# Placing rotations, a key projection, index heads and stick logits inside weight tiles of the second block's mixers

## The chip, the cores and the metric

The kernel is one program on one core of a Trainium2 chip. The metric is the device time of one execution in microseconds, the median of the runs. Everything is float32; the large products are made of float32r parts (a weight split in a high and a low part, an activation split likewise, three products summed).

## The reference, cut to what matters

Two transformer blocks of depth 2 run one after the other on 256 tokens of width 1024. The change touches the mixer of the second block (`hybrid_mixer`), which runs once for each of its two layers, between two feed-forward parts:

```python
(q_a, k_a, v_a, f_a, q_b, k_b, v_b, q_c, c_kv, q_i, k_i, w_i, gates) = split(h @ w_in)
y_a = forgetting_attention(q_a, k_a, v_a, f_a + b_forget)     # 6 heads; cumsum of log_sigmoid(f)
y_b = stick_breaking_attention(q_b, k_b, v_b)                 # 5 heads; logits z = q k^T
k_c, v_c = split(rmsnorm(c_kv, g_kv) @ w_kv_up)               # the key's up-projection
q_c, k_c = partial_rope(q_c), partial_rope(k_c)               # rotations
q_i = partial_rope(q_i)                                       # 4 index heads
k_i = partial_rope(rmsnorm(k_i, g_idx_k))                     # one index key
score = sum_h w_i[h] * relu(q_i[h] @ k_i^T)                   # index heads
y_c = attention over the top 64 keys of score (8 at a time in 8 rounds)
merged = sigmoid(gates) * (y @ w_up) ; return merged @ w_out
```

## The kernel before, in words

Features stand on the 128 partitions and tokens along the free axis. A weight piece (128 x 2048, 1 MB, or smaller) comes by DMA into one of four ring slots. ScalarE copies it in two halves to `w_hi` (float32r, two buffers; L1664), VectorE subtracts in two halves to get `ring_lo` (L2161). Both do this for the next piece when they handle the first tile of the current one (`ahead`, called at the head of `act_feat` and `dve_feat`). ScalarE may overwrite a `w_hi` buffer once TensorE has begun the piece that follows its old content.

A tile is one output chunk of 128 features by 256 tokens: 24 matmuls of 256 columns, issued by `product` (L1195) in the order 8 pairs of (high weight x high activation, high weight x low activation), then 8 of low weight x high activation. Most pieces hold two tiles. TensorE waits for `w_hi` before the first and for `ring_lo` before the 17th matmul of a tile. Tiles go to PSUM banks 0 to 2 in turn.

An ordered list of items (`add(kind, ...)`) is written out by hand. Each engine walks this one list from top to bottom and does its own part of each item: TensorE, ScalarE, VectorE and GpSimd are each strictly in that order. `fill(bank)` reserves the next use of a PSUM bank: TensorE waits in `room(f)` until the bank's former user is taken out, the engine that reads it waits in `full(f)` and counts `psum_taken` when done. Rotations, the key's up-projection (`kvup`), index heads and the head norm's sums and spread share T_BANKS (5 and 6), stick logits share S_BANKS (3 and 4).

An item with `inside=True` is left out of TensorE's walk alone; TensorE issues it instead within a tile, ahead of the matmul whose number stands in that tile's `mids`. The other engines still do it at its place in the list.

The parts of the mixer's list that matter (a chunk is a tile, `chunks(i)` a piece of two tiles):

- `chunks(0)`, `chunks(1)`: the latent, the index key, the index queries. `tok vb`: values. Then `head_squares`.
- `chunks(2)` (features 12, 13 of `q_c`), with `head_sums` between its tiles (TensorE L1442, ScalarE's root, VectorE's reciprocal L2505).
- `fox_ls`: the forget gate's log-sigmoid. VectorE adds the bias (L2640), ScalarE does Abs, Exp, Ln (L1975 to L1977), and VectorE waits for that at L2643.
- `chunks(3)`, with `head_spread` between its tiles (TensorE L1460, into both T banks; VectorE L2515).
- `chunks(4)` (QX, 9); between its tiles `kvup` (L1570, L1573), the rotations of the index key and of both index query chunks (L1470; VectorE L2526, L2527, L2529), and `key_twice` (a ScalarE copy, L1981, after the key's rotation). After its second tile four more rotations.
- the single tile of chunk 10, `index(0)`: four index heads against 128 keys (TensorE L1593, ScalarE relu L1989, VectorE L2670 and L2672).
- `chunks(5)` with `index(1)` (256 keys), the caps and stick logits 0 and 1 (`stick_z`: L1602, L1603; VectorE L2699; ScalarE Abs and Exp) between its tiles; stick logits 2 and 3 behind it; `chunks(6)` with stick logit 4 between its tiles; `chunks(7)`; `tok va` (L1426).

Of the kernel before, what the change touches and what calls it, by code (L numbers as in the profile page):

```python
# [148 lines left out]
class Plan:  # L149
# [15 lines left out]
    def linear(self):  # L165
        self.lin += 1
        if (self.lin - 1) % LIN == self.held:
            self.lin += 1
        return self.fill((self.lin - 1) % LIN)
# [10 lines left out]
    def count(self, name, n=1):  # L180
        self.counts[name] = self.counts.get(name, 0) + n
        return self.counts[name]
# [13 lines left out]
def hybrid_kernel(nc, xt, vec_d, con_d, tables_d, rpb, w, out):  # L196

    with ExitStack() as ctx:
# [399 lines left out]
                if i < len(steps) + 3:  # L598
                    g["last"] = add("att", steps=steps, i=i, inside=inside)

        def rope(chunks, block, need=(), inside=False):
            return add("rope", block=block, need=need, tb=turned_by if block == 1 else turned_by2, inside=inside,
                       chunks=[(b, a, low, linear() if inside else fill(T_BANKS[i % 2]), count("rope")) for i, (b, a, low) in enumerate(chunks)])

        def head_norm(chunks, root, kv=False, low=(0,) * 5):

# [337 lines left out]
        def second_block(l):  # L944
# [15 lines left out]
            def fc(c):  # L960
                return feats[f"2f{l}", c]

            def index(t):
                add("index", t=t, after=plan.counts["rope"], twice=plan.counts["key_twice"], fs=[fill(T_BANKS[h % 2]) for h in range(4)],
                    n=[count("relu") for _ in range(4)])

            foxes = []

# [5 lines left out]
            zs = []  # L974

            def stick_z(*hs):
                for h in hs:
                    zs.append(fill(S_BANKS[h % 2]))
                    add("stick_z", h=h, f=zs[-1], n=5 * l + h, after=fc(10))

            accs = []

# [9 lines left out]
            hn = head_norm([(feat2, CKV * S, S, v("g_kv", l), fc(CKV)), (feat2, KX * S, S, v("g_idx", l), fc(KX))], hroot2, True, (0, DH))  # L992
            head_squares(hn, 0, 1)
            t = chunks(2)
            next(t)
            head_sums(hn)
            run_all(t)
            add("fox_ls", l=l, after=feats[f"vb{l}", 0], n=count("fox_ls"))
            t = chunks(3)
            next(t)  # L1000
            head_spread(hn, 0, 1)
            run_all(t)
            t = chunks(4)
            next(t)
            kv = [fill(b) for b in (T_BANKS[0], T_BANKS[1], V_BANK)]
            add("kvup", l=l, fs=kv, need=hn["spread"][1])
            kv_last[0] = kv[-1]
            rope([(feat2, KX * S, DH), (feat2, QI * S, 0), (feat2, (QI + 1) * S, 0)], 2, need=(hn["spread"][1],))
            add("key_twice", n=plan.counts["rope"] - 2, k=count("key_twice"))
            run_all(t)  # L1010
            rope([(feat2, 12 * S, 0), (feat2, 13 * S, 0), (feat2, QX * S, DH), (kc2, 0, 0)], 2, need=(fc(QX), kv[0]))
            run_all(feat(f"2f{l}", [(0, P, cols(5, 0, P))], [10], S, length=KC * P))
            index(0)
            t = chunks(5)
            next(t)
            index(1)
            add("index_caps")
            stick_z(0, 1)
            run_all(t)
            add("index_round")  # L1020
            stick_z(2, 3)
            t = chunks(6)
            next(t)
            add("index_round")
            stick_z(4)
            run_all(t)
            add("index_round")
            t = chunks(7)
            next(t)
            add("stick_ln", n=5 * l, zs=zs)  # L1030
# [112 lines left out]
        def _(pe):  # L1143
# [21 lines left out]
            def product(fs, n, groups, fresh=None, need=None, at_col=0, mids={}, more=False, hold=False, odd=None):  # L1165

                for f in fs:
                    room(f)  # L1170
                left = [3 * sum(len(terms) for _, terms in groups)] * len(fs)
                first, at_mm = left[0], 0
                for p, terms in groups:
                    hi_w, lo_w = w_hi[p.s % 2], ring_lo[p.slot]
                    by_chunk = fresh is not None or need
                    if by_chunk:
                        order = [(*parts, t, k) for t in terms for parts in (("hi", "hi"), ("lo", "hi"), ("hi", "lo")) for k in range(len(fs))]
                    else:
                        order = [("hi", part, t, 0) for t in terms for part in ("hi", "lo")] + [("lo", "hi", t, 0) for t in terms]
                    for wpart, part, (at, hi, lo, rows, c), k in order:  # L1180
                        h = 1 if not by_chunk or at[k] + P > p.length // 2 else 0
                        for part_of, seen, ready in (("hi", hi_seen, w_hi_ready), ("lo", lo_seen, w_lo_ready)):
                            if wpart == part_of and seen.get(p.n, -1) < h:
                                seen[p.n] = h
                                pe.wait_ge(ready, 2 * p.s + h + 1)
                        if fresh is not None and wpart == "hi" and k == 0:
                            pe.wait_ge(h_hi_ready if part == "hi" else h_lo_ready, fresh - KC + c + 1)
                            if part == "lo" and c % 2 and odd is not None:
                                pe.wait_ge(odd_lo_ready, odd + c // 2 + 1)
                        if need and part == "hi" and wpart == "hi" and k == 0:  # L1190
                            pe.wait_ge(need[0], need[1] + c + 1)
                        if at_mm in mids:
                            dict(sums=pe_sums, spread=pe_spread, att=pe_att)[mids[at_mm][0]](mids[at_mm][1])
                        at_mm += 1
                        mm = pe.matmul(ps[fs[k].bank][:, at_col:at_col + n], (hi_w if wpart == "hi" else lo_w)[0:rows, at[k]:at[k] + P],  # L1195
                                       hi if part == "hi" else lo, start=left[k] == first, stop=left[k] == 1)
                        left[k] -= 1
                        if left[k] or more:
                            if not hold:
                                run(p, mm)  # L1200
                        else:
                            mm.then_inc(psum_full[fs[k].bank], 1)
# [381 lines left out]
            def pe_index(st):  # L1584
                t = st["t"]
                pe.wait_ge(rope_ready, st["after"])
                pe.wait_ge(key_twice, st["twice"])
                nk = (t + 1) * P
                for h, f in enumerate(st["fs"]):
                    room(f)  # L1590
                    a = slice(DH * (h % 2), DH * (h % 2) + DH)
                    o = (QI + h // 2) * S + t * P
                    pe.matmul(ps[f.bank][:, 0:nk], feat2[a, o:o + P], feat2[a, (KX if h % 2 else KI) * S:][:, 0:nk], start=True, stop=True)\  # L1593
                        .then_inc(psum_full[f.bank], 1)
# [544 lines left out]
        def _(dve):  # L2139
# [520 lines left out]
            def dve_index(st):  # L2660
                t = st["t"]
                nk = (t + 1) * P
                sc = score[:, t * S:t * S + nk]
                for h, (f, n) in enumerate(zip(st["fs"], st["n"])):
                    taken(f)
                    iw = vb2[:, t * 384 + 326 + h:t * 384 + 327 + h]
                    rl = relu_t[:, n % 2 * S:n % 2 * S + nk]
# [3 lines left out]
                    else:  # L2671
                        ins = dve.tensor_scalar(sc, rl, iw, None, ALU.mult)  # L2672
                    ins.then_inc(relu_used, 1)
                dve.wait_ge(relu_used, st["n"][-1])

            def by_t(do_t):
                for t in range(2):
# [173 lines left out]
```

## Time and profile before

| | us |
|---|---|
| median of 3 runs (2461.84 to 2463.28) | 2462.05 |
| the profiled execution, its own time | 2463.62 |
| its span, first to last instruction | 2461.8 |
| TensorE (PE) busy | 2410.3, 98% |
| VectorE (DVE) busy | 1557.8, 63% |
| ScalarE (ACT) busy | 1221.9, 50% |
| GpSimd (POOL) busy | 363.2, 15% |
| mean granted TensorE clock | 0.993 |

The span and the busy times are those of one profiled execution; 1.8 us of its time lie outside the span. A busy time is the union of an engine's instructions. Matmuls overlap in the records: in a stream of tiles one starts each 0.12 us and its record is 0.28 us long, so lengths of stretches are best read from starts.

### The profile page before, as it was taken

What the parts mean: (1) busy time and instruction counts of PE and PEld (TensorE: products, weight loads), DVE (VectorE), ACT (ScalarE), POOL (GpSimd) and SP (SyncE); (2) the same over time, 40 slices, a digit from 0 to 9 for tenths busy, and PEclk for the clock granted to TensorE, in tenths of its full rate; (3) what the DMA queues carried; (4) which work ended last, traced back from release to release, by engine and by line L of the source; (5) the groups of instructions that cost most, each with busy time, mean ns of one, the idle gap of its engine ahead of it and who ended that gap; (6) DMA issues with size and microseconds to landing.
All of it is one profiled execution on the core that took longest, in us unless ns stands there. A gap on an engine that the chain in (4) does not pass through costs nothing.

```text
span 2461.8 us, 36798 instructions
## 1 busy us (share of the span) xinstructions
PE 2410.3 (98%) x14494; PEld 2062.9 (84%) x14494; DVE 1557.8 (63%) x2659; ACT 1221.9 (50%) x2224; POOL 363.2 (15%) x340
## 2 busy tenths in 40 slices
PE   8999999999999999999999999999999999999998
PEld 6865678878888777888888889998888888999887
DVE  5234455663455445677678667677767767757875
ACT  4344453322223445566556545566656654547653
POOL 0333422000001325100100000240010010024000
PEclk9999999999999999999999999999999999999999
DMA  6334423444444422455555553355565564435554
GB/s 274 130 112 155 154 86 120 154 162 137 154 167 142 146 93 96 137 171 178 192 200 183 176 173 129 123 179 188 172 203 187 175 192 147 136 114 201 188 173 135
DMA packets 88603, 389.95 MB, mean 158 GB/s; under 512 B 15024, under 2 KB 27600, under 8 KB 58352
## 3 DMA queue, kind: packets, MB, share of 16 engines
q1 hardware_dynamic: 81232, 356.07, 42.5%
q0 software_dynamic: 7200, 31.52, 3.7%
q8 instruction: 116, 1.90, 0.3%
q14 instruction: 55, 0.45, 0.1%
HBM read 386.52 MB, written 1.05 MB: 157 GB/s over the span
## 4 chain that ended last, share of the span: by engine, by line
PE 90%; DVE 4%; ACT 3%; DMA 1%; issue 1%; SPq 0%; POOL 0%; DVEq 0%; POOLq 0%; ACTq 0%
PE ps L1195 40%; PE ps L1235 37%; PE ps L1426 3%; PE ps L1489 2%; PE ps L1500 2%; PE ps L1515 2%; DVE ring_lo L2161 2%; DMA prob_t<-w_mod 1%; ACT w_hi L1664 1%; PE ps L1326 1%; PE ps L1341 0%; ACT logits L1897 0%; PE ps L1470 0%; DMA ring<-w_w_in 0%; PE ps L1360 0%
## 5 line engine op out<-in xcount | busy, mean ns | idle before, releaser
L2161 DVE TENSOR_TENSOR ring_lo<-ring,w_hi 128x1024 fp32r<-128x1024 f32 (+4 forms) x708 | 774.1, 1122 | 218.7 <-ACT w_hi L1664 216.4
L1664 ACT ACTIVATE w_hi<-ring 128x1024 fp32r<-128x1024 f32 (+4 forms) x708 | 634.2, 944 | 267.9 <-PE ps L1195 175.1
L1195 PE MATMUL ps<-h_hi,w_hi 128*128 128x256 f32 (+1 forms) x1632 | 502.4, 334 | 2.4 <-issue 1.6
L1195 PE MATMUL ps<-h_lo,w_hi 128*128 128x256 f32 (+1 forms) x1632 | 489.5, 326 | 1.5 <-DVE h_lo L2334 1.5
L1235 PE MATMUL ps<-h_hi,w_hi 128*128 128x512 f32 x1760 | 449.0, 395 | 2.2 <-DVE h_hi L2334 1.8
L1235 PEld LDWEIGHTS ps<-h_hi,w_hi 128*128 128x128 f32 x1760 | 318.3, 190 | 58.6 <-issue 2.8
L1195 PEld LDWEIGHTS ps<-h_hi,w_hi 128*128 128x128 f32 x1632 | 309.0, 191 | 39.0 <-issue 12.6
L1195 PEld LDWEIGHTS ps<-h_lo,w_hi 128*128 128x128 f32 x1632 | 309.5, 191 | 25.9 <-DVE h_lo L2334 1.7
L1195 PE MATMUL ps<-h_hi,ring_lo 128*128 128x256 f32 (+1 forms) x1632 | 305.1, 325 | 2.5 <-DVE ring_lo L2161 2.5
L1195 PEld LDWEIGHTS ps<-h_hi,ring_lo 128*128 128x128 f32 x1632 | 250.5, 191 | 27.7 <-DVE ring_lo L2161 3.0
L1235 PEld LDWEIGHTS ps<-h_hi,ring_lo 128*128 128x128 f32 x1760 | 244.6, 192 | 21.7 <-DVE ring_lo L2161 3.6
L1235 PE MATMUL ps<-h_hi,ring_lo 128*128 128x256 f32 x1760 | 252.4, 284 | 2.7 <-DVE ring_lo L2161 2.7
L2088 POOL TENSOR_SCALAR logits<-logits,stat 128x512 f32<-128x512 f32 (+2 forms) x140 | 161.4, 1166 | 562.6 <-DVE stat L2571 562.6
L1235 PE MATMUL ps<-hid_both,w_hi 128*128 128x512 f32 x880 | 226.2, 393 | 0.0
L2400 DVE TENSOR_TENSOR prob_t<-ps,prob_t 128x256 f32<-128x256 f32 x260 | 110.4, 424 | 174.9 <-ACT prob_t L1810 174.6
L2044 POOL TENSOR_TENSOR logits<-logits 128x256 f32<-128x256 f32 (+1 forms) x65 | 67.7, 1041 | 1000.5 <-ACT logits L1685 781.3
L1810 ACT ACTIVATE prob_t<-ps 128x256 f32<-128x256 f32 x260 | 99.5, 383 | 213.1 <-PE ps L1235 213.1
L1235 PEld LDWEIGHTS ps<-hid_both,w_hi 128*128 128x128 f32 x880 | 161.0, 189 | 30.6
L1897 ACT ACTIVATE logits<-logits,stat 128x512 f32<-128x512 f32 (+2 forms) x140 | 81.6, 584 | 188.0 <-DVE logits L2559 93.2
L1235 PE MATMUL ps<-hid_both,ring_lo 128*128 128x256 f32 x880 | 133.4, 283 | 0.0
L1235 PEld LDWEIGHTS ps<-hid_both,ring_lo 128*128 128x128 f32 x880 | 122.5, 191 | 5.7
L1836 ACT ACTIVATE prob_t<-prob_t 128x256 f32<-128x256 f32 x110 | 46.0, 418 | 109.0 <-DVE prob_t L2424 97.2
(298 smaller groups left out, 2905.3 us busy)
## 6 DMA issues: line engine op xcount, KB each, us to landing
ring<-w_ffn_in SPq DMA_DIRECT2D x132, 1024.0 KB, 4.8
ring<-w_ffn_out SPq DMA_DIRECT2D x96, 704.0 KB, 4.1
ring<-w_in SPq DMA_DIRECT2D x36, 1024.0 KB, 4.9
ring<-w_w_in SPq DMA_DIRECT2D x26, 1024.0 KB, 4.9
bias_t<-w_mod POOLq DMA_DIRECT2D x24, 1024.0 KB, 5.4
ring<-w_mod SPq DMA_DIRECT2D x16, 1024.0 KB, 6.2
ring<-w_up SPq DMA_DIRECT2D x16, 576.0 KB, 3.8
ring<-w_pab SPq DMA_DIRECT2D x8, 1024.0 KB, 4.9
```

Of the source, the lines that this page charges most:

```text
L1195: mm = pe.matmul(ps[fs[k].bank][:, at_col:at_col + n], (hi_w if wpart == "hi" else lo_w)[0:rows, at[k]:at[k] + P], hi if part == "hi" else ...
L1235: mm = pe.matmul(ps[f.bank][:, 0:cols], wt[:, at + q * P:at + q * P + P], both[:, 0:cols], start=left[q] == n, stop=left[q] == 1, skip_gro ...
L1426: mm = pe.matmul(ps[f.bank][:, 0:st["n"]], at_T(part, c, T, t * P, P), wt[:, at:at + st["n"]], start=c == 0 and part is h_hi and not low, ...
L1489: pe.matmul(ps[f.bank][:, 0:sp_["nk"]], p["q"][a, t * P:(t + 1) * P], p["k"][a, k0:k0 + sp_["nk"]], start=True, stop=True).then_inc(psum_f ...
L1500: mm = pe.transpose(ps[f.bank][:, c * P:(c + 1) * P], logits[:, o:o + P], ident)
L1664: act.activation(w_hi[q.s % 2][:, h * n:(h + 1) * n], ring[q.slot][:, h * n:(h + 1) * n], ACT.Copy)\
L1810: act.activation(tmp[i][:, S:SQ], ps[f.bank][:, S:SQ], ACT.Copy).then_inc(half_out, 1)
L1897: act.activation(lg, lg, ACT.Exp, scale=-1.0, bias=stat[:, o:o + 1], accum_out=stat[:, 4 + o:5 + o])\
L2044: pool.tensor_tensor(sq_sum[:, o:n], sq_sum[:, o:n], sq[j % 2][:, o:n], ALU.add).then_inc(sq_added, 1)
L2088: pool.tensor_scalar(lg, lg, stat[:, 8 + (a % 2) * 2 + h:9 + (a % 2) * 2 + h], None, ALU.mult)\
L2161: dve.tensor_tensor(ring_lo[q.slot][:, c], ring[q.slot][:, c], plain(w_hi[q.s % 2][:, c]), ALU.subtract)\
L2400: dve.tensor_tensor(tmp[i][:, to:to + S], ps[f.bank][:, 0:S], tmp[i][:, S:SQ], ALU.add).then_inc(psum_taken[f.bank], 1)
```

## The change

It moves TensorE's part of these items into tiles, one or two at a stop, and with them the items' places in the list, which all engines follow:

- The rotations of the index queries go into the first tile of `chunks(2)` (ahead of matmuls 8 and 16), those of features 12 and 13 into the first tile of `chunks(3)`, `kvup` and the index key's rotation into the first tile of `chunks(4)`, those of the attention key and QX into its second tile.
- `index` now takes a list of heads: heads 0, 1 ahead of matmul 6 and heads 2, 3 ahead of matmul 16, in chunk 10's tile for the first 128 queries and in the first tile of `chunks(5)` for the others. It waits for the rotations up to the index key's alone.
- Stick logits 0, 1 go into the second tile of `chunks(5)`, 2, 3 into the first of `chunks(6)`, 4 into its second, each ahead of matmul 12.
- In the list each moved item stands ahead of its host tile's `feat` item, since it is added before `next(tile)`.
- `rope` takes the PSUM bank to use. The instructions themselves stay the same in number and shape.

```diff
-        def rope(chunks, block, need=(), inside=False):
+        def rope(chunks, block, need=(), inside=False, bank=None):
...
-            def index(t):
-                add("index", t=t, after=plan.counts["rope"], twice=plan.counts["key_twice"], fs=[fill(T_BANKS[h % 2]) for h in range(4)],
-                    n=[count("relu") for _ in range(4)])
+            def index(t, *hs):
+                return add("index", t=t, hs=hs, after=key_turned, twice=plan.counts["key_twice"], fs=[fill(T_BANKS[h % 2]) for h in hs],
+                           n=[count("relu") for _ in hs], inside=True)
+
+            def turned(chunk, bank, *need):
+                return rope([chunk], 2, need=need, inside=True, bank=T_BANKS[bank])
+
+            def among(tile, groups):
+
+                next(tile)
+                plan.items[-1]["mids"] = {at: [(it["kind"], it) for it in its] for at, its in groups.items()}
...
             t = chunks(2)
-            next(t)
+            among(t, {8: [turned((feat2, QI * S, 0), 0, fc(QI))], 16: [turned((feat2, (QI + 1) * S, 0), 1, fc(QI + 1))]})
             head_sums(hn)
             run_all(t)
             add("fox_ls", l=l, after=feats[f"vb{l}", 0], n=count("fox_ls"))
             t = chunks(3)
-            next(t)
+            among(t, {8: [turned((feat2, 12 * S, 0), 1, fc(12))], 16: [turned((feat2, 13 * S, 0), 0, fc(13))]})
             head_spread(hn, 0, 1)
             run_all(t)
             t = chunks(4)
-            next(t)
             kv = [fill(b) for b in (T_BANKS[0], T_BANKS[1], V_BANK)]
-            add("kvup", l=l, fs=kv, need=hn["spread"][1])
+            up = add("kvup", l=l, fs=kv, need=hn["spread"][1], inside=True)
             kv_last[0] = kv[-1]
-            rope([(feat2, KX * S, DH), (feat2, QI * S, 0), (feat2, (QI + 1) * S, 0)], 2, need=(hn["spread"][1],))
-            add("key_twice", n=plan.counts["rope"] - 2, k=count("key_twice"))
+            key = turned((feat2, KX * S, DH), 0, hn["spread"][1])
+            key_turned = plan.counts["rope"]
+            add("key_twice", n=key_turned, k=count("key_twice"))
+            among(t, {8: [up], 16: [key]})
+            among(t, {8: [turned((kc2, 0, 0), 1, kv[0])], 16: [turned((feat2, QX * S, DH), 0, fc(QX))]})
             run_all(t)
-            rope([(feat2, 12 * S, 0), (feat2, 13 * S, 0), (feat2, QX * S, DH), (kc2, 0, 0)], 2, need=(fc(QX), kv[0]))
-            run_all(feat(f"2f{l}", [(0, P, cols(5, 0, P))], [10], S, length=KC * P))
-            index(0)
+            among(feat(f"2f{l}", [(0, P, cols(5, 0, P))], [10], S, length=KC * P), {6: [index(0, 0, 1)], 16: [index(0, 2, 3)]})
             t = chunks(5)
-            next(t)
-            index(1)
+            among(t, {6: [index(1, 0, 1)], 16: [index(1, 2, 3)]})
             add("index_caps")
-            stick_z(0, 1)
+            among(t, {12: stick_z(0, 1)})
+            add("index_round")
+            t = chunks(6)
+            among(t, {12: stick_z(2, 3)})
+            add("index_round")
+            among(t, {12: stick_z(4)})
+            add("index_round")
             run_all(t)
-            add("index_round")
-            stick_z(2, 3)
-            t = chunks(6)
-            next(t)
-            add("index_round")
-            stick_z(4)
-            run_all(t)
-            add("index_round")
```

## Rows read from the trace of the kernel before

**Rows 1.** The page: busy time of each engine; the final chain's shares by line.
```profile
PE 2410.3 (98%) x14494; PEld 2062.9 (84%) x14494; DVE 1557.8 (63%) x2659; ACT 1221.9 (50%) x2224; POOL 363.2 (15%) x340
...
PE ps L1195 40%; PE ps L1235 37%; PE ps L1426 3%; PE ps L1489 2%; PE ps L1500 2%; PE ps L1515 2%; DVE ring_lo L2161 2%; DMA prob_t<-w_mod 1%; ACT w_hi L1664 1%; PE ps L1326 1%; PE ps L1341 0%; ACT logits L1897 0%; PE ps L1470 0%; DMA ring<-w_w_in 0%; PE ps L1360 0%
```

**Rows 2.** TensorE's waits, 1463 to 1492 us: line, releaser: us, times, longest.
```profile
PE ps L1593 <- ACT arena L1989: 0.8, 2, 0.5
PE ps L1470 <- DVE arena L2526: 0.7, 2, 0.5
```

**Rows 3.** Timeline, TensorE, layer 0's mixer: start, length, line, operands, count.
```profile
1447.86 0.28 PE L1195 MATMUL ps<-h_hi,w_hi 128*128 128x256 f32 x1
...
1457.34 0.70 PE L1460 MATMUL ps<-arena,con 32*128 32x256 f32 x4
...
1458.19 0.28 PE L1195 MATMUL ps<-h_lo,w_hi 128*128 128x256 f32 x1
...
1460.95 0.28 PE L1195 MATMUL ps<-h_hi,w_hi 128*128 128x256 f32 x1
...
1463.83 0.59 PE L1570 MATMUL ps<-arena,kvup 128*128 128x256 f32 x2
...
1499.93 0.34 PE L1426 MATMUL ps<-w_hi,h_hi 128*128 128x384 f32 x1
```

**Rows 4.** Timeline, TensorE, a rotation inside a values tile.
```profile
870.17 0.40 PE L1426 MATMUL ps<-w_hi,h_lo 128*128 128x512 f32 x1
870.41 0.59 PE L1470 MATMUL ps<-arena,tables 128*128 128x256 f32 x2
...
871.07 0.40 PE L1426 MATMUL ps<-w_hi,h_lo 128*128 128x512 f32 x1
```

**Rows 5.** Timeline, TensorE, stick logit 4 between tiles.
```profile
1489.30 1.12 PE L1195 MATMUL ps<-h_hi,ring_lo 128*128 128x256 f32 x8
1490.35 0.70 PE L1602 MATMUL ps<-arena 64*128 64x256 f32 x2
...
1491.42 0.28 PE L1195 MATMUL ps<-h_lo,w_hi 128*128 128x256 f32 x1
```

**Rows 6.** Timeline, TensorE, two heads' scores of the same shape as an index pair.
```profile
1546.00 0.70 PE L1489 MATMUL ps<-arena 64*128 64x256 f32 x4
...
1546.86 0.28 PE L1195 MATMUL ps<-h_lo,w_hi 128*128 128x256 f32 x1
```

**Rows 7.** Timeline, VectorE, layer 0's mixer (in brackets: idle before, releaser).
```profile
1450.19 2.36 DVE L2161 TENSOR_TENSOR ring_lo<-ring,w_hi 128x1024 fp32r<-128x1024 f32 x2 [2.14 <-ACT w_hi L1664]
...
1452.80 1.74 DVE L2505 RECIPROCAL arena<-arena 64x256 f32<-64x256 f32 x1
...
1454.91 0.16 DVE L2640 TENSOR_TENSOR small<-arena,vec 128x12 f32<-128x12 f32 x1
1458.50 0.17 DVE L2643 SCALAR_TENSOR_TENSOR arena<-small 128x12 f32<-128x12 f32 x1 [3.42 <-ACT small L1977]
...
1465.74 0.43 DVE L2526 TENSOR_TENSOR arena<-ps,tables 64x256 f32<-64x256 f32 x1 [0.70 <-PE ps L1470]
...
1466.99 0.42 DVE L2526 TENSOR_TENSOR arena<-ps,tables 128x256 f32<-128x256 f32 x1
```

**Rows 8.** Timeline, ScalarE, the same mixer.
```profile
1466.99 0.42 ACT L1981 ACTIVATE arena<-arena 64x256 f32<-64x256 f32 x1 [1.91 <-DVE arena L2529]
...
1478.74 2.00 ACT L1664 ACTIVATE w_hi<-ring 128x1024 fp32r<-128x1024 f32 x2
```

**Rows 9.** Stretches: from:to, us, PE busy (count), granted clock, DMA share, GB/s.
```profile
199.80:202.10 2.30, 0.07 (x3) 1.00 0.85 280
...
203.70:207.10 3.40, 3.40 (x10) 0.50 1.09 404
...
1253.20:1255.80 2.60, 0.11 (x2) 1.00 0.83 340
1255.80:1259.20 3.40, 3.40 (x21) 1.00 0.03 12
```

More of the change, by code:

```diff
@@ L599, in att @@
                     g["last"] = add("att", steps=steps, i=i, inside=inside)
-        def rope(chunks, block, need=(), inside=False):
+        def rope(chunks, block, need=(), inside=False, bank=None):
             return add("rope", block=block, need=need, tb=turned_by if block == 1 else turned_by2, inside=inside,
-                       chunks=[(b, a, low, linear() if inside else fill(T_BANKS[i % 2]), count("rope")) for i, (b, a, low) in enumerate(chunks)])
+                       chunks=[(b, a, low, fill(T_BANKS[i % 2] if bank is None else bank) if bank or not inside else linear(), count("rope")) for i, (b, a, low) in enumerate(chunks)])
         def head_norm(chunks, root, kv=False, low=(0,) * 5):
@@ L976, in stick_z @@
             def stick_z(*hs):
+                items = []
                 for h in hs:
                     zs.append(fill(S_BANKS[h % 2]))
-                    add("stick_z", h=h, f=zs[-1], n=5 * l + h, after=fc(10))
+                    items.append(add("stick_z", h=h, f=zs[-1], n=5 * l + h, after=fc(10), inside=True))
+                return items
             accs = []
@@ L1192, in product @@
                         if at_mm in mids:
-                            dict(sums=pe_sums, spread=pe_spread, att=pe_att)[mids[at_mm][0]](mids[at_mm][1])
+                            for what, it in mids[at_mm] if isinstance(mids[at_mm], list) else [mids[at_mm]]:
+                                dict(sums=pe_sums, spread=pe_spread, att=pe_att, rope=pe_rope, kvup=pe_kvup, index=pe_index,
+                                     stick_z=pe_stick_z)[what](it)
                         at_mm += 1
@@ L1588, in pe_index @@
                 nk = (t + 1) * P
-                for h, f in enumerate(st["fs"]):
+                for h, f in zip(st["hs"], st["fs"]):
                     room(f)
@@ L2663, in dve_index @@
                 sc = score[:, t * S:t * S + nk]
-                for h, (f, n) in enumerate(zip(st["fs"], st["n"])):
+                for h, f, n in zip(st["hs"], st["fs"], st["n"]):
                     taken(f)
@@ L2673, in dve_index @@
                     ins.then_inc(relu_used, 1)
-                dve.wait_ge(relu_used, st["n"][-1])
+                if st["hs"][-1] == 3:
+                    dve.wait_ge(relu_used, st["n"][-1])
             def by_t(do_t):
```

## The prediction, before the changed kernel ran

> **What bounds the kernel now.** I read the page's busy times first: TensorE works 98% of the span, and the final chain runs 77% of its time through the two tile lines [rows 1]. So time is won only where TensorE idles or loses columns, and lost as soon as it is made to wait. The second view is TensorE's waits over the stretch that the change touches: it idles 1.9 us there in each mixer, mostly for a T bank to be emptied by the rotation before or by a relu (the two rows shown make 1.5, two more 0.2 each) [rows 2]. The third is the timeline. A mixer's piece from `chunks(2)` to `tok va` lasts 1499.93 - 1447.86 = 52.07 us; a tile is 1463.83 - 1460.95 = 2.88, or 0.120 a matmul; 13 tiles make 37.44 and leave 14.63 for everything between them [rows 3]. Of that, `head_spread` costs 0.82 (its last slot before at 1457.13, second tile matmul after at 1458.19, less two ordinary slots of 0.12) [rows 3]; I estimate `head_sums`, as many instructions, at 0.75. Both stay. The six stops that the change dissolves cost 14.63 - 1.57 = 13.06. Layer 1's mixer is the same list, so all is counted twice.
>
> **What the moved matmuls cost inside tiles.** None is removed. A 128-row rotation inside a tile takes 871.07 - 870.17 = 0.90, less two slots of 0.23 there, 0.44 [rows 4]; I use 0.43, its columns alone. Five of them: 2.15. `kvup` I keep at 0.82. Stick logit 4 alone costs 1491.42 - 1490.14 (the start of the eighth `ring_lo` matmul) - 0.24 = 1.04, for 0.64 of columns (384, four passes at 2.4 GHz): a spell of 64-row operands in the stream costs 0.40 extra [rows 5]. No row shows a 64x64 rotation alone: from 0.54 (its pitch in a row of rotations) to 0.43 + 0.40 = 0.83; I take 0.83, nearest to how it will stand, for two 1.66. An index pair of 256 keys costs 0.83 by the score pair of the same shape, of 128 keys 0.21 less [rows 6]: four make 2.9. Stick logits 1.5, 1.5 and 1.04: 4.0. Sum 11.5. Bounds: 11.2 with the cheap rotation, and 12.4 from the other side (13.06 less the 1.9 of waits, plus three more 64-row spells at 0.40, six before and nine after). Taken: **-1.6 us a mixer** (-0.7 to -1.9).
>
> One rule speaks against the change. The Trainium skill, TensorEngine Tiling (Array Packing), Key Properties, says that a change of tiling mode drains TensorE. The 0.40 in rows 5 against nothing extra in rows 4 agrees with it. With switches free inside tiles, a mixer would be 3.6 cheaper still, and the result about 7 us lower.
>
> **What the new order makes late.** The moved items stand ahead of their host's `feat` item, so on VectorE and ScalarE they come before the next piece's split.
>
> (1) *`head_spread` waits for both T banks, and these now hold the rotations of features 12 and 13.* VectorE does these behind `fox_ls`, where it already sits idle 3.42 us for ScalarE's chain [rows 7]. That chain now starts later: the two index rotations in `chunks(2)` come first on VectorE. The second is issued at 1447.86 + 16 slots + 0.43 = 1450.21, done on TensorE about 0.6 later, and VectorE needs 1.2 for a rotation (1465.74 to 1466.99) [rows 7], so it is free at 1452.1 for the `ring_lo` that began at 1450.19. Everything behind it (two evictions, the 1.74 reciprocal, the bias add at 1454.91, the return at 1458.50) moves by 1.9: VectorE comes back at 1460.4, does rotation 12 from 1460.6 and the first operation of 13 from 1461.8, and bank 5 is free at 1462.25. TensorE reaches `head_spread` at 1457.34 + 4 x 0.43 = 1459.06. It waits **3.2 us**. Before, nothing on TensorE waited for `fox_ls`. Bounds 2.9 and 3.5 (rotations of 1.1 or 1.25 us).
>
> (2) *QX.* From the slot k of the key's rotation: TensorE done at k+0.74; VectorE from +0.87 to +2.1; then `key_twice`, which followed at once before (0.42) [rows 8], and only then ScalarE's split of chunk 10 (two halves of 0.6), to k+3.6; VectorE's second half, then QX's eviction, out at k+4.7. TensorE wants QX at k + 0.83 + 8 slots + 16 slots + 0.43 = k+4.1. Wait **0.7** (0.4 to 1.0).
>
> (3) *`w_hi` of `chunks(5)`.* ScalarE did this split (2.00 us [rows 8]) as chunk 10's tile began; now four relus come first. From the slot s of heads 2, 3: TensorE done at s+0.57, two relus to s+1.0, both halves at s+3.0. TensorE wants them at s + 0.61 + 8 slots = s+1.57. Wait **1.5** (1.3 to 1.7). The same order in the first tile of `chunks(5)` costs nothing, since the second tile's 2.88 + 1.5 hide it. `chunks(7)`'s split, behind stick logits 2 and 3 on ScalarE, has about 1 us in hand, and `tok va`'s about 0.4; for its second piece, where TensorE idles 0.55 already, I add **0.2**.
>
> Sum: -1.6 + 3.2 + 0.7 + 1.5 + 0.2 = **+4.0 a mixer, +8.0**. DMAs, SP and GpSimd: no transfer is moved; the ring's only get more time, and GpSimd has no part in the moved items.
>
> (4) *The clock.* After TensorE stood almost idle for 2.3 us at 199.8, the granted clock was 0.50 from 203.7 to 207.1; after a pause as long at 1253.2 it stayed 1.00 [rows 9]. Of the five pauses or clusters with over 2 us idle in this trace four were followed by such a spell. Pauses of 1 to 1.6 us mostly were not. A 3.2 us wait is longer than any single one so far, so I count a spell in each mixer. 3.4 us at 1.2 GHz hold 16 tile matmuls (256 columns: 0.213) where 28 would fit at 0.120: 1.5 us lost, **+3.0** for two. Bounds: none (0) and two a mixer (+6).
>
> Total 8.0 + 3.0 = 11 us. Against the profiled execution: 2463.62 + 11 = 2474.6. The median of the runs shown is 1.6 lower, so **2473.0**.
>
> **Rivals.**
> - *The waits, but no low clock* (or one spell in all): 2470 to 2471.5. For it: the pause at 1253. Against: the other four.
> - *More is late*: a second spell after the 1.5 us wait, or `chunks(7)`'s split misses its 1 us: 2475 to 2478. For it: one pause of only 1.04 us near 1238 preceded a spell. Against: six of 1.1 to 1.6 didn't.
> - *Other side: VectorE gets to rotations 12 and 13 in time.* One mechanism: the T banks are empty when TensorE reaches `head_spread` at 1459.06. It needs `fox_ls` to return before 1457.2 instead of 1460.4, by having its chain overlap. Then the 3.2 and the clock spells fall away, and if the relus also run ahead so that (3) hides, only -1.6 + 0.7 a mixer is left: 2460; with all waits gone, 2459. For it: the 1.9 us of waits before really go [rows 2]. Against: VectorE's idle 3.42 stands in the list between the two [rows 7], and the point is missed by 3 us.
> - *The waits are half of what I count* (say (1) at 1.5 with no spell, (3) at 1): about 2462 to 2465, near no change. For it: my sums chain many steps. Against: each is in-order work with durations from rows.
>
> **How the numbers follow.** The forecast (three waits, a spell in each mixer) 0.45; no or one spell 0.24; more late 0.09; near no change 0.12; the other side 0.10. About 0.2% (4.9 us) is what a measurement of this kernel tells from none: 2457.1 to 2467.0. Slower: 0.45 + 0.24 + 0.09 = 0.78; same: 0.12 and half of the other side, whose 2459 to 2460 lies within, 0.17; faster, where more waits go than I see, 0.05. The range runs from 2466, under the no-spell case with the waits at their low bounds, to 2477, the forecast with one more spell or the high bounds; it leaves out about 2 in 10.
>
> **What would show it.** In the changed kernel's timeline: TensorE idle about 3 us ahead of `head_spread`, released by VectorE's rotation (L2526's successor); 0.7 ahead of QX's rotation, released by its eviction; 1.5 ahead of the first tile of `chunks(5)`, released by ScalarE's `w_hi`. The mixer's stretch goes from 52.1 to some 56, or 57.6 with a spell; the mean granted clock falls by two spells in 2462 us, about 0.001. The old waits at the rotations, relus and stick logits are gone. If `head_spread` starts without a wait, the main step is wrong; if TensorE waits there but the clock stays 1.00, only (4) is.

## The result, and the profile after

| | before | after |
|---|---|---|
| median of 5 runs each, us | 2463.28 (2461.84 to 2463.81) | 2471.3 (2469.98 to 2474.19) |
| ratio, with its 95% interval | | 1.0038 [1.0027, 1.0049] |
| the profiled execution, its own time, us | 2463.62 | 2471.3 |
| span, us | 2461.8 | 2469.5 |
| mean granted TensorE clock | 0.993 | 0.992 |

The changed kernel is slower by 8.0 us by the medians (6.7 to 12.1 by the interval of the ratio) where 11 were forecast. Its median lies 1.7 us under the predicted 2473.0 and inside the range.

On the page TensorE's busy time barely moves (2410.3 before, 2411.9 here), so the page alone does not show what the change did [rows 1]:

```profile
PE 2411.9 (98%) x14494; PEld 2062.4 (84%) x14494; DVE 1555.3 (63%) x2659; ACT 1221.2 (49%) x2224; POOL 363.6 (15%) x340
```

The length to compare is a mixer's stretch: the time from its first matmul of `tok vb` to its first of `tok va`, in layer 0 and in layer 1. First the kernel before, then the changed one (us; busy PE, PEld, DVE, ACT, POOL; granted clock, DMA share, GB/s):

```profile
1440.50:1499.93 59.43, 57.56 (x426) 52.78 (x425) 44.14 (x91) 31.46 (x52) 0.00 (x0) 1.00 0.44 142
```

```profile
1437.68:1502.05 64.37, 59.02 (x426) 53.73 (x425) 43.65 (x90) 30.70 (x52) 0.00 (x0) 0.97 0.41 131
2047.47:2111.83 64.36, 59.01 (x426) 53.72 (x425) 43.64 (x90) 30.71 (x52) 0.00 (x0) 0.97 0.41 131
```

The stretch grew by 4.94 us. TensorE is idle for 5.35 us of it (64.37 - 59.02) instead of 1.87, and the granted clock fell from 1.00 to 0.97. TensorE's waits in layer 0, over 1445 to 1510 (as [rows 2]; total us, times, longest):

```profile
PE ps L1469 <- DVE arena L2535: 2.8, 1, 2.8
PE ps L1204 <- ACT w_hi L1673: 1.4, 1, 1.4
PE ps L1435 <- ACT w_hi L1673: 1.2, 2, 0.9
PE ps L1479 <- issue: 0.9, 1, 0.9
```

The old waits on rotations, relus and the stick bank are gone, as the new list intended; four groups stand in their place. TensorE's timeline says where (start us, length; as [rows 3]; idle before and releaser in brackets):

```profile
1459.12 0.48 PE L1469 MATMUL ps<-arena,con 32*128 32x256 f32 x2 [2.84 <-DVE arena L2535]
1472.09 0.61 PE L1479 MATMUL ps<-arena,tables 64*64 64x256 f32 x2 [0.85 <-issue]
1479.28 0.36 PE L1204 MATMUL ps<-h_hi,w_hi 128*128 128x256 f32 x1 [1.37 <-ACT w_hi L1673]
1502.05 0.41 PE L1435 MATMUL ps<-w_hi,h_hi 128*128 128x384 f32 x1 [0.28 <-ACT w_hi L1673]
```

They are `head_spread`, QX's rotation, the first tile of `chunks(5)` and `tok va`, whose second piece waits another 0.93 (0.55 before). What `head_spread` waits for is on VectorE (as [rows 7]):

```profile
1451.85 1.73 DVE L2514 RECIPROCAL arena<-arena 64x256 f32<-64x256 f32 x1
1453.79 0.15 DVE L2649 TENSOR_TENSOR small<-arena,vec 128x12 f32<-128x12 f32 x1
1457.36 0.17 DVE L2652 SCALAR_TENSOR_TENSOR arena<-small 128x12 f32<-128x12 f32 x1 [3.42 <-ACT small L1986]
1457.47 0.42 DVE L2535 TENSOR_TENSOR arena<-ps,tables 128x256 f32<-128x256 f32 x1
1458.60 0.41 DVE L2535 TENSOR_TENSOR arena<-ps,tables 128x256 f32<-128x256 f32 x1
```

VectorE adds the forget gate's bias, stands idle 3.42 us for ScalarE's chain (Abs, Exp, Ln), and only then reads the two rotations. The idle has the length it had before; what is new is that T banks, and so TensorE, hang on it. Most of the 3.42 us is two loads of function tables on ScalarE, one ahead of Exp and one ahead of Ln:

```profile
1454.20 1.28 ACT L1985 ACT_TABLE_LOAD   x1
1455.72 1.28 ACT L1986 ACT_TABLE_LOAD   x1
```

TensorE's pause and what the clock did behind it, the second of these in both mixers:

```profile
1456.28:1459.12 2.84, 0.01 (x1) 0.04 (x1) 1.73 (x6) 2.83 (x4) 0.00 (x0) 1.00 0.18 75
1459.84:1463.25 3.41, 3.41 (x16) 3.41 (x17) 3.38 (x5) 0.00 (x0) 0.00 (x0) 0.50 0.02 5
2070.80:2074.20 3.40, 3.40 (x18) 3.40 (x17) 2.41 (x5) 0.00 (x0) 0.00 (x0) 0.50 0.00 0
```

TensorE ran 3.4 us at 1.2 GHz (granted clock 0.50) with hardly a gap: 16 matmuls where 28 fit at 2.4 GHz. Such a time at the low clock is called a spell below. It is the one part of the loss that no list of waits shows.

### The profile page after: what moved, and what is told of

The parts are those of the page before. It is cut to its first block, busy times and chain, and to the rows that moved or that the text cites. A ratio compares the mean times of both kernels' runs of the same rounds, so it can differ in the third digit from the quotient of the medians.

```text
span 2469.5 us, 36830 instructions
## 1 busy us (share of the span) xinstructions
PE 2411.9 (98%) x14494; PEld 2062.4 (84%) x14494; DVE 1555.3 (63%) x2659; ACT 1221.2 (49%) x2224; POOL 363.6 (15%) x340
## 3 DMA queue, kind: packets, MB, share of 16 engines
HBM read 386.52 MB, written 1.05 MB: 157 GB/s over the span
## 4 chain that ended last, share of the span: by engine, by line
PE 89%; ACT 4%; DVE 4%; DMA 1%; issue 1%; SPq 0%; POOL 0%; DVEq 0%; ACTq 0%; POOLq 0%
PE ps L1204 40%; PE ps L1244 37%; PE ps L1435 3%; PE ps L1498 2%; PE ps L1509 2%; PE ps L1524 2%; DVE ring_lo L2170 2%; DMA prob_t<-w_mod 1%; ACT w_hi L1673 1%; PE ps L1335 1%; PE ps L1350 0%; ACT logits L1906 0%; PE ps L1479 0%; DMA ring<-w_w_in 0%; PE ps L1272 0%
```

## The experiments

Each diff is against the changed kernel unless the text says otherwise, with `...` for what is left out and notes behind `#` that the kernels do not have. "The chain" is the forget gate's work: VectorE's bias add; ScalarE's Abs, Exp and Ln; VectorE's last step. A "split" is ScalarE's copy of a weight piece to `w_hi` with VectorE's subtraction behind it. The times compared are each version's median and that of the kernel before, run beside it. Stretches are given as layer 0 / layer 1; 64.37 / 64.36 is the changed kernel's.

**e1_fox_late** takes the forget gate's chain out from in front of the rotations.

```
-            add("fox_ls", l=l, after=feats[f"vb{l}", 0], n=count("fox_ls"))     # behind chunks(2)
...
             among(t, {12: stick_z(0, 1)})
+            add("fox_in", l=l, after=feats[f"vb{l}", 0], n=count("fox_ls"))     # bias add, Abs, Exp
...
+            add("fox_out", n=plan.counts["fox_ls"])                             # Ln, last step; behind tok va
```

> Theory (VectorE stands for the forget gate's chain in front of rotations 12 and 13, and head_spread's banks hang on them): with the forget gate's work moved in the list to behind the stick logits, TensorE's 2.84 us wait ahead of head_spread goes in both mixers, no wait takes its place at kvup (spread 1 is out about 0.5 us before), and the low clock spells right after it go too. 2 x (2.84 + 1.5) = 8.7 us less than the changed kernel's 2471.3: about 2462.6, ratio to before near 1.000. The waits of 0.85 (QX) and 1.37 (w_hi) stay. Rival (the stops inside tiles themselves are what costs, through changes of operand shape): the wait goes but little is won, 2469 or more. Rival (the forget gate's chain is needed where it is and its later place delays something else): a new wait of 1 us or more between chunks(5) and the gates.

Measured: 2465.0 us against 2462.26, ratio 1.0014 [1.0005, 1.0022]; stretches 60.47 / 60.46, clock 1.00, no wait at `head_spread`. The 2.84 us wait and the spell go with the chain, so that is shown. The time is 2.4 us above the 2462.6 expected. The gain is 3.9 us a mixer where the 2.84 idle and 1.5 of clock make 4.3: the second row of its waits over 1480 to 1510 shows what came back, a wait of 0.5 ahead of `chunks(7)` for its split.

```profile
PE ps L1436 <- ACT w_hi L1674: 1.2, 2, 0.9
PE ps L1205 <- ACT w_hi L1674: 0.5, 1, 0.5
```

ScalarE's timeline shows where the 0.5 comes from: the chain's Abs and Exp now stand among those of the stick logits, ahead of that split.

```profile
1485.68 0.20 ACT L1985 ACTIVATE small<-small 128x12 f32<-128x12 f32 x1
1485.91 0.21 ACT L1986 ACTIVATE small<-small 128x12 f32<-128x12 f32 x1
1486.16 0.53 ACT L2007 ACTIVATE prob_t<-logits 128x384 f32<-128x384 f32 x1
```

They take 1486.16 - 1485.68 = 0.48 us, and the split begins 5.67 us behind the first stick logit's Abs where it was 5.18 in the changed kernel. The rows also show a gain: the Exp needs no table load here, as the stick logits' Exp has just been done. The profile of the changed kernel has 36 table loads, that of e1 32, two fewer in each mixer.

**e2_own_banks** leaves the chain where it is and gives rotations 12 and 13 two other banks, so `head_spread` has nothing to wait for.

```
-                                      16: [turned((feat2, 13 * S, 0), 0, fc(13))]})
+                                      16: [turned((feat2, 13 * S, 0), 0, fc(13), banks=S_BANKS)]})   # and 12 likewise
```

> Rotations 12 and 13 write banks 4 and 3, which nothing else uses then, in place of the T banks; VectorE's list is as in the changed kernel. Theory (VectorE standing in its list is the cause, the bank only the place where it shows): head_spread starts without a wait, but kvup, which needs the spread that VectorE applies after the two rotations, the split and an eviction, waits about 3.0 us instead, again with a low clock spell behind it: total 2470 to 2472, no gain. Rival (the shared banks are the cause): the wait goes and nothing replaces it, 2462.6.

Measured: 2472.62 against 2462.26, ratio 1.0043 [1.003, 1.0056]; stretches 64.81 / 64.83. `head_spread` starts at once, and nothing is won:

```profile
1464.43 0.48 PE L1579 MATMUL ps<-arena,kvup 128*128 128x256 f32 x1 [2.44 <-DVE arena L2524]
```

```profile
1461.90:1464.40 2.50, 0.09 (x1) 0.00 (x0) 2.44 (x5) 0.00 (x0) 0.00 (x0) 1.00 0.90 265
1465.40:1472.20 6.80, 6.80 (x29) 5.82 (x28) 2.48 (x5) 1.95 (x6) 0.00 (x0) 0.50 0.00 1
```

The wait moved to `kvup`, which needs VectorE's product with the spread, again behind the chain. It is 0.4 shorter, QX's wait of 0.85 is gone, and the spell is twice as long, 6.8 us, which takes back more than both. So the banks were only where TensorE met VectorE's delay; the cause is VectorE's standing.

**e3_spin** fills the wait with matmuls nobody reads: 12 of a 128x128 block of ones (two records each), ahead of `head_spread`.

```
+            add("spin", f=Fill(S_BANKS[1], plan.taken[S_BANKS[1]], 0, 0))
             head_spread(hn, 0, 1)
...
+                room(f)
+                for _ in range(12):
+                    pe.matmul(ps[f.bank][:, 0:P], ones[:, :], ones[:, :], start=True, stop=True)
```

> Twelve unread 128-column matmuls of ones (2.7 us) into the free bank 4 ahead of head_spread in both mixers; the wait on the banks stays, but TensorE is busy in it. Theory (the low clock spell follows TensorE's idleness and costs 1.5 us each): head_spread starts at the same time, the spells in the two mixers are gone (granted clock 1.00 there) and the time is 3.0 us less, 2468.3. Rival (the spells have another cause, or cost nothing as later waits hide them): time as in the changed kernel, 2471.3.

Measured: 2469.18 against 2462.26, ratio 1.0027 [1.0017, 1.0038]; stretches 62.88 / 62.87.

```profile
1457.87 2.84 PE L1257 MATMUL ps<-ones 128*128 128x128 f32 x24
1460.87 0.70 PE L1476 MATMUL ps<-arena,con 32*128 32x256 f32 x4 [0.16 <-issue]
```

The time in which TensorE can't go on is the same, but the clock stays at 1.00 behind it. 64.37 - 62.88 = 1.49 us a mixer is thus the price of the spell alone (forecast 1.5). The medians of two different sets of runs differ by 2.1 us (2471.3 and 2469.18) where this makes 3.0.

**e4_all_three** is e1 and the two other orders: `key_twice` stands behind the tile that hosts `kvup` and the key's rotation, so that ScalarE splits chunk 10 first; and index heads 2 and 3 stand behind their host tile, so that ScalarE splits `chunks(5)` after two relus, not four.

```
-            add("key_twice", n=key_turned, k=count("key_twice"))
             among(t, {8: [up], 16: [key]})
+            add("key_twice", n=key_turned, k=count("key_twice"))
...
-            among(feat(...), {6: [index(0, 0, 1)], 16: [index(0, 2, 3)]})
+            first = index(0, 0, 1)
+            among(feat(...), {6: [first]})
+            host = plan.items[-1]
+            host["mids"][16] = [("index", index(0, 2, 3))]
```

> The forget gate late as in e1, key_twice behind QX's tile in the list, and the index heads 2, 3 of the first 128 queries behind chunk 10's tile in the list (TensorE's own order as in the changed kernel). Theory: all three waits go (2.84, 0.85, 1.37 us a mixer) and the spells with them: 2471.3 - 8.7 - 1.7 - 2.7 = 2458.2, ratio to before 0.998. Rival (stops inside tiles cost themselves): not faster than before, 2463 or more.

Measured: 2458.61 against 2462.26, ratio 0.9987 [0.9978, 0.9995]; stretches 57.98 / 57.97. All that is left to wait for is ahead of `chunks(7)` and in `tok va`; over 1430 to 1510:

```profile
PE ps L1439 <- ACT w_hi L1677: 1.2, 2, 0.9
PE ps L1208 <- ACT w_hi L1677: 0.5, 1, 0.5
```

**e6_index_order** and **e8_twice_order** do one of the two orders alone, with the chain left in its place.

> The changed kernel with one list place changed: index heads 2, 3 of the first 128 queries behind chunk 10's tile. Theory: the 1.37 us wait on w_hi ahead of chunks(5) goes, the stretch from tok vb to tok va goes from 64.37 to 63.0, the time to 2468.6. Rival: the relus of heads 2, 3 come late and the T banks are not free at the next index heads, so the wait only moves: 64.4, 2471.3.

Measured: 2469.19 against 2461.18, ratio 1.0032 [1.002, 1.0043]; stretches 62.72 / 64.26. The wait of 1.37 is gone and the others stay. Layer 0 gains 1.65; layer 1 gains almost nothing, because its spell was 6.8 us this time and not 3.4, behind the same wait of 2.8.

> The changed kernel with one list place changed: key_twice (ScalarE's copy of the turned index key) behind QX's tile. Theory: the split of chunk 10 no longer stands behind the key's rotation, QX is evicted in time, the 0.85 us wait ahead of QX's rotation goes; stretch 64.37 to 63.4, time 2469.4. Rival: QX waits for VectorE's own three rotation operations, not for the split: wait of 0.5 us or more left.

Measured: 2472.85 against 2461.18, ratio 1.0044 [1.003, 1.0057]; stretches 63.61 / 64.98. QX's 0.85 is gone, so ScalarE's `key_twice` ahead of the split was its cause, though the profile puts it down to "issue". `chunks(5)` then waits 1.51 instead of 1.37, and layer 1 again has a 6.8 us spell. So the two stretches together gain 0.1 where the order is worth 0.8 in each: one longer spell took the rest. The median is 3.5 us above the 2469.4 expected, and 2.5 above that of e10, the changed kernel again. The profiles place this ahead of the mixers, in code that is the same in both: e8's enters the first mixer at 1441.30 and e10's at 1436.65, and from there to the end e8's takes 0.6 us less (1031.38 and 1031.94).

**e7_before_fox_late** is the kernel before with the chain's two parts moved as in e1.

> The kernel before, all stops between tiles as they were, with the forget gate's work moved behind the stick logits as in e1. Theory (VectorE's standing for it was free there, since no rotation stood behind it): the stretch from tok vb to tok va stays at 59.4 (59.2 to 59.8), ratio 1.000. Rival (e1's and e4's gain is the forget gate's own, two table loads and 3.4 us of VectorE's standing, and has nothing to do with the rotations' place): 2 us or more faster than before.

Measured: 2462.07 against 2461.18, ratio 1.0 [0.9991, 1.0009]; stretches 59.45 / 59.46. VectorE's standing of 3.42 us, and with it the two table loads that go here too, was free before, since no bank waited on it. It became a cost by the new order alone. The chain's new place has a price of its own: the wait in `tok va`, behind the stretch, is 0.91 here and was 0.55.

**e5_best** was meant to remove the 0.5 ahead of `chunks(7)` (2457 expected): e4 with stick logits 2, 3 and 4 also created behind their host tiles and the chain's first part behind those.

```
+            for hs in (2, 3), (4,):
+                among(t, {})
+                host = plan.items[-1]
+                host["mids"][12] = [("stick_z", it) for it in stick_z(*hs)]
+                add("index_round")
```

> e4 with two more list places changed: stick logits 2, 3 and 4 stand behind their host tile's item, so ScalarE splits chunks(7) first, and the forget gate's first part stands behind stick logit 4. Theory: of e4's waits (0.50 ahead of chunks(7), 0.28 and 0.93 in tok va) the 0.50 and 0.28 go and the 0.93 falls to 0.55 or less. The stretch from tok vb to tok va, 57.98 us in e4 and 59.42 before, becomes 57.0 to 57.3; 4.5 to 6 us less than before in all, 2457, ratio 0.998. Rival (ScalarE is simply full here and a split moved forward only delays the Abs and Exp that the logits need): a new wait of 0.3 us or more at stick logits or tok va, no gain on e4.

Measured: 2465.41 against 2461.18, ratio 1.0015 [1.0006, 1.0025]; stretches 61.19 / 61.19, longer than e4's by 3.2. First TensorE, then VectorE:

```profile
1493.54 0.45 PE L1616 MATMUL ps<-arena 64*128 64x256 f32 x1 [2.85 <-DVE logits L2719]
```

```profile
1490.23 2.36 DVE L2177 TENSOR_TENSOR ring_lo<-ring,w_hi 128x1024 fp32r<-128x1024 f32 x2 [2.31 <-ACT w_hi L1678]
1492.51 0.42 DVE L2403 SCALAR_TENSOR_TENSOR arena<-ps,row 128x256 f32<-128x256 f32 x1
1492.84 1.01 DVE L2719 TENSOR_TENSOR logits<-ps,tables 128x384 f32<-128x384 f32 x2
```

The mistake is the same as the change's: the stick logits that free stick logit 4's bank now stand on VectorE behind a split, and VectorE first stands 2.31 us for ScalarE and then splits for 2.36. TensorE waits 2.85, and a spell of 3.4 follows.

**e9_best2** is e4 with the chain's first part ahead of `chunks(5)`, and stick logit 4's tile directly behind that of 2 and 3.

> e4 with two list places changed: the forget gate's first part ahead of chunks(5), where ScalarE and VectorE have time, and stick logit 4 with its tile ahead of the index round that stood between it and stick logit 3; stick logits 2 and 3 stay ahead of their host tile. Theory (e5's new 2.85 us wait came from VectorE reaching stick logit 2 only behind a split and an eviction, with its bank held; and e4's 0.50, 0.28 and 0.93 from ScalarE's splits standing behind this work): none of e4's waits is left above 0.3 us, no wait at stick logit 4, stretch from tok vb to tok va 57.98 to 57.0 to 57.4, some 0.6 more saved within tok va; 5 to 6 us less than before in all, ratio 0.9975 to 0.998. Rival (these waits only move): stretch 57.9 or more, time as e4, ratio 0.9987.

Measured: 2460.86 against 2461.2, ratio 0.9997 [0.9988, 1.0006]; stretches 60.44 / 58.92. The waits at `chunks(7)` and in `tok va` are gone, but no time was won where 5 to 6 us were expected: a wait of 1.88 is new, at index heads 2 and 3 of `chunks(5)`. Its cause is on ScalarE:

```profile
1477.56 0.21 ACT L1988 ACTIVATE small<-small 128x12 f32<-128x12 f32 x1 [2.41 <-DVE small L2655]
1477.79 1.28 ACT L1989 ACT_TABLE_LOAD   x1
1479.33 0.66 ACT L2004 ACTIVATE arena<-ps 128x256 f32<-128x256 f32 x2
```

ScalarE waits 2.41 us for VectorE's bias add, does Abs, loads a table for 1.28 and has two relus late. The windows over the pause and behind it:

```profile
1478.00:1479.90 1.90, 0.04 (x1) 0.07 (x1) 0.15 (x1) 1.86 (x4) 0.00 (x0) 1.00 0.44 184
1480.00:1483.40 3.40, 3.40 (x14) 2.75 (x15) 2.23 (x5) 2.48 (x4) 0.00 (x0) 0.51 0.03 5
```

Layer 1, with the same wait, had no spell: 60.44 - 58.92 = 1.52 is the clock's price once more.

**e10_after_again** is the changed kernel unaltered, beside other runs of the kernel before.

> The changed kernel unchanged, beside the same runs of before. Waits of 2.84, 0.85 and 1.37 us and a low clock spell behind the first in each mixer as in its first profile, ratio to before 1.003 to 1.005.

Measured: 2470.39 against 2461.2, ratio 1.0036 [1.0023, 1.005]; stretches 64.36 / 64.36.

**e11_best3** places each part of the chain in a hole (idle time of the engine that does it) of e9's trace: the bias add behind `head_squares`, ahead of `chunks(2)`; Abs and Exp behind the first tile of `chunks(3)`, where ScalarE has nothing to do before the split of `chunks(4)`.

```
             head_squares(hn, 0, 1)
+            add("fox_x", l=l, after=feats[f"vb{l}", 0])                         # VectorE's bias add
...
             among(t, {8: [turned((feat2, 12 * S, 0), 1, fc(12))], 16: [turned((feat2, 13 * S, 0), 0, fc(13))]})
+            add("fox_in", n=count("fox_ls"))                                    # ScalarE's Abs, Exp
             head_spread(hn, 0, 1)
```

> e9 with the forget gate's first part placed by the trace: VectorE's bias add ahead of chunks(2), where its operand has long been there, and ScalarE's Abs and Exp behind the first tile of chunks(3), where ScalarE idles over 6 us in e9; Ln and VectorE's last step stay behind tok va. Theory: e9's 1.88 us wait at the index heads goes with the 0.9 that it adds around it, nothing takes its place (no wait above 0.4 us in the mixer), no low clock spell there. Stretch from tok vb to tok va, 58.92 us in e9's undisturbed mixer and 59.42 before, becomes 56.1 to 56.5; 6 to 7.5 us less than before in all, 2454 to 2456, ratio 0.997 to 0.9975. Rival (some wait always forms, since all engines' work is fixed and this stretch is full): stretch 57.5 or more, ratio above 0.9985.

Measured: 2455.52 (2454.52 to 2457.91) against 2463.2, ratio 0.9967 [0.9955, 0.9979]. The stretch in both layers, then the chain's parts on VectorE and ScalarE in layer 0:

```profile
1440.97:1497.79 56.82, 56.82 (x426) 52.13 (x425) 43.75 (x89) 29.18 (x50) 0.00 (x0) 1.00 0.47 149
2042.40:2099.20 56.80, 56.80 (x426) 52.11 (x425) 43.73 (x89) 29.16 (x50) 0.00 (x0) 1.00 0.48 149
```

```profile
1449.14 0.17 DVE L2656 TENSOR_TENSOR small<-arena,vec 128x12 f32<-128x12 f32 x1 [0.58 <-ACT arena L1809]
```

```profile
1456.10 2.01 ACT L1678 ACTIVATE w_hi<-ring 128x1024 fp32r<-128x1024 f32 x2 [2.77 <-PE ps L1209]
1458.01 0.20 ACT L1989 ACTIVATE small<-small 128x12 f32<-128x12 f32 x1
1458.23 1.28 ACT L1990 ACT_TABLE_LOAD   x1
1459.52 0.21 ACT L1990 ACTIVATE small<-small 128x12 f32<-128x12 f32 x1
```

TensorE is busy 56.82 of 56.82 us. This version beats both kernels: 7.7 us under the one before and, by the two ratios to it, 0.7% under the changed one. Everything the change placed inside tiles is still there; only four pieces of ScalarE's and VectorE's work around it stand elsewhere (the chain, `key_twice`, index heads 2 and 3, stick logit 4). No run gives the last three their new places with the stops between tiles, so how much of the gain they would bring there is not shown.

## Why the prediction was right

*The stops, forecast -1.6 a mixer.* The direction was right, the size too small. Read from the slots around them (less 0.24), the moved matmuls cost: five 128-row rotations 0.43 each (forecast 0.43), `kvup` 0.87 (0.82), the key's 64x64 rotation 0.76 (0.83), index pairs 0.61 and 0.82 (as forecast), stick logit 4 1.04 (as forecast), and the two stick pairs 1.05 each where 1.5 was taken. A pair costs what one head costs alone. The rows of stick logits 2 and 3, with the last tile matmul before them and the first two behind:

```profile
1489.11 0.28 PE L1204 MATMUL ps<-h_lo,w_hi 128*128 128x256 f32 x1
1489.32 0.71 PE L1611 MATMUL ps<-arena 64*128 64x256 f32 x4
1489.85 0.39 PE L1612 MATMUL ps<-arena 64*128 64x128 f32 x4
1490.18 0.39 PE L1204 MATMUL ps<-h_hi,w_hi 128*128 128x256 f32 x1
1490.40 0.28 PE L1204 MATMUL ps<-h_lo,w_hi 128*128 128x256 f32 x1
```

Eight records take 1490.40 - 1489.11 - 0.24 = 1.05 us, where stick logit 4's four take 1.04. In the kernel the two heads of a pair read opposite halves of the partitions (`DH * (h % 2)`, DH = 64), and the rows have eight records in the time of four: the two run side by side. Both index pairs fit the same sum, one head's columns and 0.40 (0.21 + 0.40 and 0.43 + 0.40), so the forecast's price of an index pair held already what its price of a stick pair lacked. In the kernel before, the second head waited 0.21 us for its bank, and that stop cost 1.76 in all.

QX's rotation is 0.76 too without its wait. All of it, without the waits, sums to 2.15 + 0.87 + 1.52 + 1.22 + 1.64 + 2.10 + 1.04 = 10.54 us, against 13.12 in the kernel before, its 1.87 of waits included: -2.6, of which 1.0 was missed. 0.9 of that are the stick pairs, taken at 1.5 with no row that shows a pair alone. The bound of -1.9 left that price fixed, and so was too narrow: the step came out beyond it. e11 confirms the size without waits to disturb it: 59.43 - 56.82 = 2.61.

*The mode change.* The Trainium skill, TensorEngine Tiling (Array Packing), Key Properties, says that a change of tiling mode drains TensorE. The trace after agrees in that the 64x64 rotation costs 0.76 inside a tile, 0.33 more than a 128-row one of as many columns. That a tile doesn't hide it was said in the forecast and held.

*(1) `head_spread`, forecast 3.2 (2.9 to 3.5).* 2.84, just under the lower bound, released by VectorE's first operation of rotation 13 as predicted. With the 2.82 us by which this profile enters the mixer earlier, TensorE came to `head_spread` at 1456.28 + 2.82 = 1459.10 (forecast 1459.06), VectorE back at 1460.18 (1460.4), and the second bank was free at about 1461.9 (1462.25). e1, e2 and e7 show the cause from three sides: without the chain no wait, with other banks the same delay one step on, and no cost in the old order.

*(2) QX, forecast 0.7.* 0.85; e8 shows `key_twice` ahead of the split as its cause. *(3) `chunks(5)`, forecast 1.5.* 1.37; e6 shows the order of relus and split as its cause.

*`tok va`, forecast +0.2.* +0.38 in the second piece (0.93 for 0.55), and 0.28 at the first, which before didn't wait: the "0.4 in hand" was none. `chunks(7)` had its split in time in the changed kernel, as said, but not with "about 1 us in hand": ScalarE's second half ends at 1495.64 and TensorE begins the piece at 1495.79. So the 0.48 us that e1 put ahead of this split became a wait of 0.5.

*(4) The clock, forecast 1.5 a mixer.* A spell in each mixer, 1.49 by e3, as forecast. That both were 3.4 us long is in part luck: e6 and e8 have the same wait of 2.8 us in both mixers, and in each of them one spell of the two was 6.8 us long.

*The sum.* The waits cost their recorded idle and some 0.05 to 0.25 around each: 3.01 + 0.90 + 1.61 + 0.5 = 6.0. With the stops and the spell, -2.58 + 6.0 + 1.49 = +4.9, the 4.94 measured; with `tok va`'s second piece 5.3 a mixer, 10.6 for two, where 11 was forecast. So two sizes were off, the stops by 1.0 and the waits by about 0.8, and they nearly cancel. The close total is luck; the waits, their places and their releasers are not.

*The rest.* The medians differ by 8.0 and, in e10, by 9.2, not by 10.6. The profiles meet the sum once the code ahead of the mixers, which is the same in all kernels, is left out. From the first matmul of the first mixer's `tok vb` to the end of the span, in the kernel before, the changed kernel and e10:

```profile
1440.50:2461.80 1021.30, 1003.93 (x6712) 911.17 (x6710) 741.44 (x1348) 573.74 (x1051) 110.30 (x123) 1.00 0.49 165
1437.68:2469.50 1031.82, 1007.10 (x6712) 912.98 (x6710) 740.53 (x1348) 573.07 (x1051) 110.77 (x123) 0.99 0.49 163
1436.65:2468.60 1031.95, 1007.25 (x6712) 913.08 (x6710) 740.61 (x1348) 573.10 (x1051) 110.76 (x123) 0.99 0.49 163
```

That is 10.5 and 10.6 us more. For e1, e2, e7, e8 and e11 this length, too, is within 0.5 us of what their stretches and `tok va`'s second wait make (2.8, 11.5, 0.8, 10.5 and -6.3); for e3, e4, e5, e6 and e9 it is 0.6 to 1.3 less. In e3, with 1.3, the low clock that ends every profile begins 5.5 us before the end, and 8.7 in the kernel before.

Most of the scatter lies ahead: over the thirteen profiles the first mixer is entered between 1436.05 (e1) and 1441.94 (e5), with 13.6 us at the low clock before it in e1 and 27.3 in e5. The medians stand on both sides of the sums: e2 1.2, e3 0.7, e4 1.5 and e11 1.3 better, e5 1.6 and e8 1.2 worse, and the medians of the kernel before itself run from 2461.18 to 2463.28. So differences of 1 to 2 us between these medians carry no argument here. Why the spells ahead of the mixers differ from one execution to the next stays open.

*The rival cases.* No spell (2470 to 2471.5) holds the measured time by its number, but not by its mechanism: the clock rows show the spell in both mixers. The other side, the banks empty in time, gave 2459 to 2460; e4, which builds that by moving the chain and the two orders, has 2458.61. *More is late* did not occur: no spell follows the wait of 1.37. *Half the waits* is excluded by their measured lengths.

## What to carry to other kernels

Where in-order engines walk one list, the place of an item is set for the engine that stands longest at it: before work is moved behind a place at which VectorE or ScalarE idles, ask which bank or buffer that idle time will now hold; an idle engine is free only until something is queued behind it. Giving the waiting matmul another bank doesn't help when the engine behind it is late (e2); moving the cause does, and it has to go into a hole that the trace shows on each engine it touches (e11, after e5 and e9 missed one). Where ScalarE's function changes, the place also decides on a table load of 1.28 us (e1). Two matmuls of 64 rows on opposite halves of the partitions are to be issued together, since here the second cost nothing. And a wait of 2 to 3 us on TensorE is to be priced with its spell of low clock, here half as much again.

## What the runs showed of the hardware

- A spell at 1.2 GHz came after pauses of TensorE of 2.84, 2.85 and 2.44 us in every mixer that had one, and after one of 1.88 us in one mixer of two (e9). Behind the wait of 2.84 it was 3.4 us long in six mixers of eight (the changed kernel, e10, layer 0 of e6 and e8) and 6.8 us in two (layer 1 of e6 and e8). The short one cost 1.49 us (e3), the long one 1.4 to 1.5 us more (e6 and e8, layer 1 against layer 0).
- Unread matmuls in the pause kept the clock at 1.00 (e3), and were worth 1.49 us a mixer though they do no work.
- A 128-row float32 rotation of 256 columns inside a tile of float32r matmuls cost 0.43 us, one of 64 rows 0.76. Stick logit 4, of 64 rows, cost the same 1.04 inside a tile as between two.
- Two 64-row heads on opposite partition halves, issued one behind the other, cost what one costs: 1.05 us for a pair of stick logits against 1.04 for one.
- A table load took 1.28 us on ScalarE, six times as long as the activation of 12 columns behind it (0.21). The chain had two where it stood alone, one ahead of its Exp in e9 and e11 (where the stick logits' Exp then needed none), and its Exp had none between the stick logits' (e1, e4).
